# Three 192-byte gaps in SBUF ahead of stationary operands of a three-block transformer kernel

## The chip, the cores and the metric

The kernel runs on one core of one Trainium2 chip. The metric is device time in microseconds (us) from start to end of one execution; the kernel before takes 1477.13 us, the median of three runs (1477.1 to 1477.38).

## The reference, cut to what matters

The input is x, 256 tokens by 1024 channels, float32. Two layers of a first block and one second block are applied:

```
for l in 0, 1:
    x += 0.5 * rms(swiglu(rms(x), w_gu, w_down))     # 1024 -> 2*2816 -> 1024
    x += rms(hybrid_mixer(rms(x)))                   # projections, RG-LRU branch, SSD branch, gated branch, then @ w_out
    x += 0.5 * rms(swiglu(rms(x), w_gu2, w_down2))
x += (g0*y_ssm + g1*y_conv + g2*y_attn) @ w_out      # second block, "mixed" = the bracket
x += swiglu(rms(x), w_gu3, w_down3)
```

So there are five feed-forward parts, two hybrid mixers and one mixer of the second block. Every weight is read once, 480 chunks of 128 x 1024 float32.

## The kernel before, in words

Products are made in the float32r form. To keep float32 accuracy each operand is split in two, hi and lo, and a product is three matmuls: hi x hi, hi x lo, lo x hi (`product`, lines 475 to 477). SyncE brings the weight chunks in a fixed order into a ring of six slots (`raw`), ScalarE rounds each to `whi` (line 454), VectorE makes `wlo = raw - whi` (line 461), and TensorE uses them; a slot is given back by the semaphore `consumed`.

A matmul has a stationary operand, loaded into the array by a weight load (LDWEIGHTS, "PEld" in the profile), and a moving operand that streams through, up to 512 columns. The weight load of the next matmul runs beside the current matmul. In the profile's names `out<-moving,stationary` the moving operand stands first.

- Gate and up columns (`columns_of`, lines 762 and 763): the weights are stationary, the normalized input `xboth` moves. For each of 8 blocks k one matmul with 512 columns and one with 256. A hidden tile j has one gate chunk and one up chunk, so 32 matmuls; 20 tiles of each feed-forward part are made so, the first two in another form (`head`).
- Down products (`down`, `first_down`, and `held` for the last four): the hidden activations `hhi`, `hlo` are stationary (128 x 128), the weights move with 512 columns, into `acc`. 12 matmuls for a tile; 18 tiles of each part stand between gate-and-up groups, the last four make one run of 48.
- Output product of the hybrid mixer: the stationary operand is `yahi`, `yalo` for the three blocks of the recurrent branch (36 matmuls) and the two halves of `xboth` for the other five (60), `left(k, t)`; the weights move with 512 columns.
- Output product of the second block: stationary `mxhi`, `mxlo` (96 matmuls), moving weights, 512 columns.
- Token projections (`tokens`): stationary `xboth`, moving weights. Channel projections (`channels`): stationary weights, moving `xboth`, 256 columns.

The order of the work on each engine is written out by hand; the FFN tiles 6 to 17 stand in a loop of each engine, the rest is unrolled.

SBUF tensors are placed one after another in the order of their declaration. `m1` declares tensors of a scope; when a scope is closed, the next declaration starts again where that scope began. So `hhi` (first scope), `recc` (second scope) and `y5hi` (third) start at the same byte. The program's addresses in a partition, modulo 128:

```
tensor                    before   after
raw, whi, wlo, xboth         0       0
x, xn, u32                   0       0
hhi, hlo, rrow              64       0
recc, xbcc, par, xdt        64      64
yahi, yalo                  64       0
dm, yb, yc, vx               0      64
y5hi, y5lo, cvhi, cvlo      64      64
ohi, olo                    64      64
mxhi, mxlo, gsg, sgl, mt    64       0
```

Within a tensor all stationary blocks lie at multiples of 512 bytes, and a moving operand of 512 columns starts at a multiple of 1024 bytes.

Of the kernel before, what the change touches and what calls it, by code (L numbers as in the profile page):

```python
# [18 lines left out]
P = 128  # L19
# [16 lines left out]
HEADS = 6  # L36
HD = 64
VSTEPS = 49

FFN_CHUNKS = 3 * FT  # L40
MIX_CHUNKS = 30
# [164 lines left out]
def block_program(nc, stream, x_in, pf_a, pf_b, pm, pm2, out):  # L206
    ctx = ExitStack()
    with ctx:
        def sb(name, shape, dt=F32):
            return ctx.enter_context(nc.sbuf_tensor(name, shape, dt))  # L210
# [35 lines left out]
        def m1(name, shape, dt=F32):  # L246
            return scope.enter_context(nc.sbuf_tensor(name, shape, dt))

        hhi = m1("hhi", [P, HELD, S], F32R)
        hlo = m1("hlo", [P, HELD, S], F32R)  # L250
        rrow = m1("rrow", [P, S])
# [9 lines left out]
        uv = m1("uv", [P, T, 2 * CW])  # L261
        zs = m1("zs", [P, T, BW])
        xdt = m1("xdt", [P, T, BW])
        yahi, yalo = m1("yahi", [P, AB, S], F32R), m1("yalo", [P, AB, S], F32R)
        spin = m1("spin", [P, T * HEADS + AB])
        spe = m1("spe", [P, T * HEADS + AB])
# [63 lines left out]
        ohi, olo = sb("ohi", [P, 4, S], F32R), sb("olo", [P, 4, S], F32R)  # L330
        gx = sb("gx", [P, 4, S])
        gates32 += [gx[:, j, :] for j in range(3)] + [xn[:, t, 512:768] for t in range(T)] + [xn[:, 0, 768:D]]
        mxhi, mxlo = sb("mxhi", [P, KD, S], F32R), sb("mxlo", [P, KD, S], F32R)
        gsg, sgl = sb("gsg", [P, 2, 3, S]), sb("sgl", [P, 2, S])
        mt = sb("mt", [P, 3, S])
# [45 lines left out]
        def mixsig(name, per):  # L381
            mixsigs[name] = Signal(sem("m_" + name), per)
            return mixsigs[name]
# [34 lines left out]
        wst = mixsig("wst", 1)  # L418
        vstep = mixsig("vstep", VSTEPS)

# [2124 lines left out]
```

## Time and profile before

| | |
|---|---|
| median of three runs | 1477.13 us (1477.1 to 1477.38) |
| span of the profiled execution | 1475.7 us; its whole time is not listed apart, the median is 1.4 us above the span |
| PE (matmul) busy | 1459.6 us, 99%, 8583 matmuls |
| PEld (weight load) busy | 1268.2 us, 86% |
| VectorE busy | 1148.6 us, 78% |
| ScalarE busy | 766.9 us, 52% |
| granted TensorE clock | 0.995 of full speed |
| DMA | 261.75 MB, 177 GB/s |

The recorded end of a matmul is modelled and matmuls overlap in the records, so the busy time says only that TensorE never paused. What a matmul costs is read from the distance between the starts of two neighbours in the timeline.

### The profile page before, as it was taken

To read this page: it belongs to the slowest core of one execution; us is meant where nothing else is said; L and a number is where in the kernel's file an instruction comes from. 1 tells how busy PE (TensorE), PEld (TensorE's weight loads), DVE (VectorE), ACT (ScalarE), POOL (GpSimd) and SP (SyncE) were. 2 spreads that over 40 slices of the span, in tenths; PEclk is the share of its full clock that TensorE was granted. 3 is DMA by queue.
4 is the path that set the end of the run, shared out by engine and by line. 5 is a ranking of instruction groups with operands and counts; after the bars stand their busy time and mean duration, and the time that the engine had idled before them with its cause. 6 is when DMAs were issued, how large, how long until landed. Compare 5 with 4: busy or idle time off the path is not lost.

```text
span 1475.7 us, 24487 instructions
## 1 busy us (share of the span) xinstructions
PE 1459.6 (99%) x8583; PEld 1268.2 (86%) x8583; DVE 1148.6 (78%) x1831; ACT 766.9 (52%) x1252; POOL 144.1 (10%) x140
## 2 busy tenths in 40 slices
PE   8999999999999999999999999999999999999999
PEld 7888889888888888889988888889988899888887
DVE  5777777878777777777787777868999977577876
ACT  6343465663434544337655434468598665453432
POOL 0000015100000000002420000020433310000000
PEclk9999999999999999999999999999999999999999
DMA  8565545546655666655545655555522256556662
GB/s 317 195 202 190 186 168 172 161 152 194 198 183 194 213 201 201 186 188 167 159 158 182 200 197 186 198 172 182 175 72 88 87 182 187 173 164 197 195 191 80
DMA packets 71361, 261.75 MB, mean 177 GB/s; under 512 B 8048, under 2 KB 8048, under 8 KB 71024
## 3 DMA queue, kind: packets, MB, share of 16 engines
q1 hardware_dynamic: 69984, 253.79, 53.6%
q10 hardware_dynamic: 1296, 6.85, 1.3%
q8 instruction: 55, 0.90, 0.3%
q14 instruction: 26, 0.21, 0.0%
HBM read 259.56 MB, written 1.05 MB: 177 GB/s over the span
## 4 chain that ended last, share of the span: by engine, by line
PE 92%; DVE 4%; ACT 2%; issue 1%; POOL 0%; DMA 0%; ACTq 0%; DVEq 0%
PE work L762 25%; PE work L763 13%; PE acc L475 9%; PE acc L477 9%; PE acc L476 9%; PE work L475 8%; PE work L477 7%; PE work L476 7%; DVE wlo L461 2%; PE work L1494 1%; PE acc L1523 1%; ACT whi L454 1%; PE acc L1559 1%; PE work L1495 0%; PE work L1019 0%
## 5 line engine op out<-in xcount | busy, mean ns | idle before, releaser
L461 DVE TENSOR_TENSOR wlo<-raw,whi 128x1024 fp32r<-128x1024 f32 x460 | 550.8, 1224 | 179.7 <-ACT whi L454 178.6
L762 PE MATMUL work<-xboth,whi 128*128 128x512 f32 x1600 | 560.8, 394 | 0.0
L454 ACT ACTIVATE whi<-raw 128x1024 fp32r<-128x1024 f32 x480 | 475.9, 1040 | 60.9 <-PE work L477 35.9
L763 PE MATMUL work<-xboth,wlo 128*128 128x256 f32 x1600 | 444.3, 278 | 0.0
L762 PEld LDWEIGHTS work<-xboth,whi 128*128 128x128 f32 x1600 | 299.8, 187 | 69.3
L763 PEld LDWEIGHTS work<-xboth,wlo 128*128 128x128 f32 x1600 | 300.8, 188 | 4.3
L840 ACT ACTIVATE sg<-sg 128x256 f32<-128x256 f32 x100 | 41.8, 418 | 476.0 <-DVE sg L881 476.0
L477 PE MATMUL acc<-whi,hlo 128*128 128x512 f32 x440 | 173.7, 395 | 0.0
L476 PE MATMUL acc<-wlo,hhi 128*128 128x512 f32 x440 | 173.5, 394 | 0.0
L475 PE MATMUL acc<-whi,hhi 128*128 128x512 f32 x440 | 173.3, 394 | 0.0
L475 PE MATMUL work<-xboth,whi 128*128 128x256 f32 x416 | 120.1, 289 | 0.0
L476 PE MATMUL work<-xboth,whi 128*128 128x256 f32 x416 | 118.5, 285 | 0.0
L477 PE MATMUL work<-xboth,wlo 128*128 128x256 f32 x416 | 118.4, 285 | 0.0
L475 PEld LDWEIGHTS acc<-whi,hhi 128*128 128x128 f32 x440 | 82.4, 187 | 20.0
L477 PEld LDWEIGHTS acc<-whi,hlo 128*128 128x128 f32 x440 | 82.4, 187 | 19.9
L476 PEld LDWEIGHTS acc<-wlo,hhi 128*128 128x128 f32 x440 | 82.4, 187 | 15.8
L475 PEld LDWEIGHTS work<-xboth,whi 128*128 128x128 f32 x416 | 80.7, 194 | 0.5 <-issue 0.4
L476 PEld LDWEIGHTS work<-xboth,whi 128*128 128x128 f32 x416 | 80.6, 194 | 0.1
L477 PEld LDWEIGHTS work<-xboth,wlo 128*128 128x128 f32 x416 | 80.5, 194 | 0.0
L475 PE MATMUL work<-whi,xboth 128*128 128x512 f32 (+3 forms) x208 | 77.3, 371 | 2.9 <-DVE xboth L537 2.1
L543 POOL TENSOR_TENSOR prstd<-pms,small 128x1 f32<-128x1 f32 x12 | 6.6, 551 | 740.4 <-DVE pms L551 740.4
L879 DVE TENSOR_REDUCE sg<-work 128x256 f32<-128x512 f32 x100 | 68.7, 687 | 11.5 <-PE work L763 11.4
(438 smaller groups left out, 2193.5 us busy)
## 6 DMA issues: line engine op xcount, KB each, us to landing
raw<-stream SPq DMA_DIRECT2D x480, 512.0 KB, 3.7
par<-pm ACTq DMA_DIRECT2D x2, 1644.5 KB, 7.3
pfa<-pf_a ACTq DMA_DIRECT2D x3, 516.0 KB, 4.7
pfb<-pf_b ACTq DMA_DIRECT2D x2, 516.0 KB, 8.2
x<-x_in SPq DMA_DIRECT2D x2, 512.0 KB, 6.0
out<-x SPq DMA_DIRECT2D x4, 256.0 KB, 2.0
par<-pm ACTq DMA_DIRECT2D x1, 820.0 KB, 4.3
pre<-pf_a ACTq DMA_DIRECT2D x1, 4.0 KB, 4.3
```

Source lines behind the costliest of these rows:

```text
L454: nc.scalar.activation(chunk(whi, place, c)[:, cols], chunk(raw, place, c)[:, cols], ACT.Copy).then_inc(hi_ready, 1)
L461: nc.vector.tensor_tensor(chunk(wlo, place, c)[:, cols], chunk(raw, place, c)[:, cols], chunk(whi, place, c)[:, cols].bitcast(F32), ALU.su ...
L475: return [nc.tensor.matmul(o, lhi, rhi, start=start, stop=False), nc.tensor.matmul(o, lhi, rlo, start=False, stop=False), nc.tensor.matmul ...
L476: nc.tensor.matmul(o, lhi, rlo, start=False, stop=False),
L477: nc.tensor.matmul(o, llo, rhi, start=False, stop=stop)]
L762: nc.tensor.matmul(o[:, :], hi[:, k * P:(k + 1) * P], xboth[:, k, :], start=k == 0, stop=False)
L763: m = nc.tensor.matmul(o[:, 0:S], lo[:, k * P:(k + 1) * P], xhi[:, k, :], start=False, stop=k == KD - 1)
L840: nc.scalar.activation(sg[:, j % 2, :], sg[:, j % 2, :], ACT.Silu).then_inc(sg_ready, 1)
L879: nc.vector.tensor_reduce(sg[:, j % 2, :], both_halves(gate), AX.X, ALU.add).then_inc(gsum_ready, 1)
L1494: nc.tensor.matmul(bank2(f"sc{r}", slice(b * S, b * S + nkeys(t))), qT[:, h, t * P:(t + 1) * P], kT[:, 2 * b + h // 4, 0:nkeys(t)], start= ...
L1523: m = nc.tensor.matmul(acc[at:at + 32, 1, k % 2 * S:(k % 2 + 1) * S], left, rotated[:, r % 2, i // 2, i % 2, :], start=i == 0, stop=i == 3)
L1559: m = nc.tensor.matmul(acc[:, 0, at:at + HD], pT[:, r % 2, (b * 2 + k) * P:(b * 2 + k + 1) * P], xn[:, k, 768 + b * P + (h // 4) * HD:768 ...
```

## The change

Three unused tensors of 48 float32 (192 bytes in each partition) are declared, one ahead of `hhi`, one ahead of `yahi`, and one ahead of `mxhi`. No instruction is added, removed or moved; the tensors declared after a gap in the same scope (and, for the last, to the end) start 192 bytes later.

```diff
+LINE = 48
...
+        m1("hidden_line", [P, LINE])
         hhi = m1("hhi", [P, HELD, S], F32R)
         hlo = m1("hlo", [P, HELD, S], F32R)
         rrow = m1("rrow", [P, S])
...
         xdt = m1("xdt", [P, T, BW])
+        m1("lru_line", [P, LINE])
         yahi, yalo = m1("yahi", [P, AB, S], F32R), m1("yalo", [P, AB, S], F32R)
...
         gates32 += [gx[:, j, :] for j in range(3)] + [xn[:, t, 512:768] for t in range(T)] + [xn[:, 0, 768:D]]
+        sb("mixed_line", [P, LINE])
         mxhi, mxlo = sb("mxhi", [P, KD, S], F32R), sb("mxlo", [P, KD, S], F32R)
         gsg, sgl = sb("gsg", [P, 2, 3, S]), sb("sgl", [P, 2, S])
         mt = sb("mt", [P, 3, S])
```

## Rows read from the trace of the kernel before

**Rows 1.** Windows: length, then busy us (count) of each engine, clock, DMA.
```profile
core 0: us, PE busy (x) PEld busy (x) DVE busy (x) ACT busy (x) POOL busy (x), PEclk, DMA share, GB/s
22.00:195.00 173.00, 173.00 (x921) 148.40 (x921) 134.54 (x193) 73.28 (x94) 0.55 (x1) 1.00 0.61 201
```

**Rows 2.** Timeline of VectorE, one FFN tile: start us, length; idle before.
```profile
338.64 1.23 DVE L461 TENSOR_TENSOR wlo<-raw,whi 128x1024 fp32r<-128x1024 f32 x1 [1.43 <-ACT whi L454]
```

**Rows 3.** Timeline of PE: a gate-and-up group, then a down tile.
```profile
330.39 0.40 PE L762 MATMUL work<-xboth,whi 128*128 128x512 f32 x1
...
335.94 0.39 PE L475 MATMUL acc<-whi,hhi 128*128 128x512 f32 x1
336.17 0.39 PE L476 MATMUL acc<-wlo,hhi 128*128 128x512 f32 x1
...
338.74 0.40 PE L762 MATMUL work<-xboth,whi 128*128 128x512 f32 x1
```

**Rows 4.** Timeline of PE: a token projection of 48, stationary xboth; then channels.
```profile
1004.91 0.40 PE L475 MATMUL work<-whi,xboth 128*128 128x512 f32 x1
...
1006.07 0.39 PE L477 MATMUL work<-whi,xboth 128*128 128x512 f32 x1
...
1015.82 0.28 PE L475 MATMUL work<-xboth,whi 128*128 128x256 f32 x1
1015.93 0.28 PE L476 MATMUL work<-xboth,whi 128*128 128x256 f32 x1
1016.05 0.28 PE L477 MATMUL work<-xboth,wlo 128*128 128x256 f32 x1
```

**Rows 5.** Timeline of PE: last xboth matmul, then the 36 with stationary yahi, yalo.
```profile
272.97 0.39 PE L476 MATMUL work<-wlo,xboth 128*128 128x512 f32 x1
273.19 0.39 PE L477 MATMUL work<-whi,xboth 128*128 128x512 f32 x1
273.42 0.40 PE L475 MATMUL acc<-whi,yahi 128*128 128x512 f32 x1
...
281.82 1.89 PE L1056 MATMUL work<-vx,par 128*128 128x64 f32 x16
```

**Rows 6.** Timeline of PE: 39 of the matmuls with stationary mxhi, mxlo.
```profile
1263.03 0.39 PE L475 MATMUL acc<-whi,mxhi 128*128 128x512 f32 x1
...
1272.13 0.39 PE L475 MATMUL acc<-whi,mxhi 128*128 128x512 f32 x1
```

**Rows 7.** Groups of PE by form: count, busy us, mean ns of one, idle.
```profile
L475 PE MATMUL acc<-whi,hhi 128*128 128x512 f32 x440 | 173.3, 394 | 0.0
L475 PE MATMUL acc<-whi,yahi 128*128 128x512 f32 x24 | 9.5, 396 | 0.0
L475 PE MATMUL acc<-whi,mxhi 128*128 128x512 f32 x32 | 12.7, 397 | 0.0
L762 PE MATMUL work<-xboth,whi 128*128 128x512 f32 x1600 | 560.8, 394 | 0.0
```

**Rows 8.** Timeline of PE: ten matmuls of the mixer's output, from its second.
```profile
288.62 0.40 PE L476 MATMUL acc<-wlo,xboth 128*128 128x512 f32 x1
...
290.71 0.39 PE L476 MATMUL acc<-wlo,xboth 128*128 128x512 f32 x1
```

**Rows 9.** Timeline of PE: after the gated branch, a wait inside the mixer's output product.
```profile
285.14 0.47 PE L475 MATMUL acc<-whi,xboth 128*128 128x512 f32 x1 [0.76 <-DVE xboth L1326]
```

**Rows 10.** Groups by form: operands behind a gap, and two without a gap.
```profile
L1043 PE MATMUL acc<-xdt,dm 128*128 128x64 f32 x24 | 4.5, 270 | 0.0
L1065 PE MATMUL work<-ident,yb 128*128 128x128 f32 x12 | 1.6, 274 | 0.0
L1012 PE MATMUL work<-ident,xbcc 128*128 128x128 f32 x12 | 1.6, 272 | 0.0
```

**Rows 11.** Timeline of PE: up columns of the second feed-forward part, before its first down tile.
```profile
316.76 0.40 PE L762 MATMUL work<-xboth,whi 128*128 128x512 f32 x1
317.01 0.28 PE L763 MATMUL work<-xboth,wlo 128*128 128x256 f32 x1
317.13 0.40 PE L762 MATMUL work<-xboth,whi 128*128 128x512 f32 x1
317.36 0.28 PE L763 MATMUL work<-xboth,wlo 128*128 128x256 f32 x1
...
318.88 0.40 PE L762 MATMUL work<-xboth,whi 128*128 128x512 f32 x1
```

## The prediction

> **What bounds the kernel now.** I read the page's busy line first: PE is busy 99% of the span. Since the end of a matmul is modelled, this proves little alone, so I next took the windows: in 173 us of a feed-forward part PE is busy all 173.00 [rows 1], while VectorE works 134.5 us of it and ScalarE 73.3. VectorE idles 1.43 us in every tile of about 8.35 us, waiting for ScalarE's split [rows 2], so it has slack in each. So in the feed-forward parts TensorE sets the pace, and an engine that hides the effect isn't there: what a matmul gives back, the kernel gets.
>
> The third view is the timeline, read for the distance between starts. A 512-column matmul cannot start its successor earlier than its columns stream. The reader is to see three distances for the same kind of matmul (stationary 128 x 128 activations, moving weights, 512 columns, granted clock 1.00):
> - stationary `hhi`, `hlo`: a down tile starts at 335.94, its second matmul at 336.17, the next group at 338.74 [rows 3]. That is 2.80 us for 12, 0.230 for the first and 2.57 / 11 = 0.2336 for each other.
> - stationary `yahi`, `yalo`: 36 in 281.82 - 273.42 = 8.40 us, 0.2333 each [rows 5]; stationary `mxhi`, `mxlo`: 39 in 9.10 us, 0.2333 each [rows 6].
> - stationary `xboth`: the last 43 of a run of 48 take 1015.82 - 1006.07 = 9.75 us, 0.2267 each [rows 4]. Right ahead of the `yahi` matmuls, two starts lie 0.22 and 0.23 apart [rows 5].
>
> The first two groups lie 64 bytes off the weights modulo 128, `xboth` lies at 0 like them. Nothing else that I can find separates them, except that `xboth` stands at a lower address. So 6.7 ns (0.2333 - 0.2267) of each such matmul hang on the placement, and the change moves all three to 0.
>
> **The change part by part.** The gaps add no instruction, no DMA and no wait. The sum is one of matmul distances.
>
> 1. *Down tiles.* The three groups with stationary `hhi`, `hlo` have 440 each (one of them stands in [rows 7]), 1320 matmuls in all: 90 tiles of 12 and 5 runs of 48. At 0.2267 a tile takes 2.720 us instead of 2.80 (2.797 by 0.230 + 11 x 0.2333), so at most 0.077 is saved. But `xboth` doesn't start at 0.2267: the first five of the run of 48 take 1006.07 - 1004.91 = 1.16 us, 0.232 each [rows 4], a toll of 5 x 0.2320 - 5 x 0.2267 = 0.027 us. Whether a down tile, which follows gate-and-up matmuls, pays it isn't shown: bounds 0 and 0.027 per tile (0.050 for the nine at 0.232 after a pause [rows 8], see the rivals). TensorE comes from stationary weights at 0 as in the run of 48, but in another rhythm, and the first matmul already takes 0.230; I take half, 0.013. A tile saves 0.064, 90 save 5.8 us (bounds 4.5 and 6.9).
> 2. *The five runs of 48.* Each saves 47 x 0.0067 = 0.315 less 0.013, so 0.30; five save 1.5 us.
> 3. *Recurrent output.* 3 x 24 matmuls [rows 7] x 0.0067 = 0.48 us. They follow a settled `xboth` run, so no toll. But 1.9 us of gated products and the transposes come next, and then TensorE waits 0.76 us for VectorE [rows 9]. If VectorE's chain starts from TensorE's gated products, it comes earlier too; if from its own older work, the wait grows and the gain is nil. Bounds 0 and 0.48; I take 0.24.
> 4. *Mixed output.* 3 x 32 matmuls [rows 7] x 0.0067 - 0.027 = 0.6 us, with nothing waited for inside the run.
> 5. *Tensors pushed the other way.* `dm`, `yb`, `yc` and `vx` go from 0 to 64. They are stationary operands of 64 and 128 columns, where the weight load sets the distance. The nearest rows: transposes with stationary `yb` at 0 and `xbcc` at 64 take 274 and 272 ns, and the products with `dm` at 0 take 270 [rows 10]. I take 0; at 6.7 ns each, all 124 of them (72 `dm`, 32 `vx`, 20 `yb` and `yc`) would be 0.8 us either way.
> 6. `rrow`, `gsg`, `sgl`, `mt` are read by VectorE and ScalarE alone. I take nothing; both have slack, as above.
>
> Sum: 5.8 + 1.5 + 0.24 + 0.6 = 8.1 us. The profiled span is 1475.7 us and would be 1467.6; the median stands 1.4 us above the span, so the time is 1477.1 - 8.1 = 1469.0 us. Its own range: without tolls 6.9 + 1.6 + 0.5 + 0.6 = 9.6 us, 1467.5; with the whole toll everywhere and nothing for part 3, 4.5 + 1.4 + 0.6 = 6.5 us, 1470.6; with the 0.8 of part 5 either way, 1466.7 to 1471.4.
>
> **The rivals.**
>
> *Gate-and-up falls into its slower rhythm (slower).* The 512/256 pair of gate and up has two rhythms in this trace. Normally a group takes 335.94 - 330.39 = 5.55 us for 16 pairs, 0.347 a pair [rows 3]. Ahead of the first down tile of a feed-forward part, six pairs take 318.88 - 316.76 = 2.12 us, 0.353 a pair, with 0.25 in place of 0.23 at every third 512-column matmul [rows 11]. Both operands are at 0 there too, so a rhythm depends on how the group is entered, and it persists once begun. All 90 groups that follow a down tile with `hhi` at 64 show the fast one (95 of the 100 hidden tiles that the 1600 pairs [rows 7] make, since the last group of each part holds two). The change replaces exactly what comes ahead of them. If the new entry gives the slow rhythm, 0.0067 x 16 pairs = 0.107 us is lost in each of 95 tiles, 10.2 us, against 8.1 won: 1479.2 us; with the full toll on the down tiles (6.5 won) 1480.8. It decides from 76 slow tiles on. For it: of the ten 16-matmul halves made before the first down tile, five are slow. Against: channel projections that follow settled `xboth` runs come to their usual 0.12 at the second matmul [rows 4].
>
> *The tolls eat most.* If a down tile needs nine matmuls at 0.232, as the run that begins after a pause does (290.71 - 288.62 = 2.09 us for nine [rows 8]), a tile saves 2.797 - 9 x 0.232 - 3 x 0.2267 = 0.029, 90 save 2.6 us, the long runs 5 x 0.265 = 1.3, the rest 0.7: 4.6 us in all, 1472.5 us. Against: that run begins when no weight was loaded ahead, which isn't so for a down tile.
>
> *The placement isn't the cause.* Then the lower address, or the tensor's neighbourhood, makes `xboth` fast, and the distances stay: 1477.1 us. For it: `hhi`, `yahi` and `mxhi` all lie at high addresses, so phase and region aren't told apart by the rows. Against: three tensors far from each other cost the same 0.2333, and all share the phase 64.
>
> The Trainium skill speaks for this last outcome too: "TensorE: Matmul & The Clock Gate", Part 2, says that TensorE has two independent read ports of SBUF, one for the moving operand and one for the weight load, so that loading the next weights takes nothing from the running matmul. By it no placement of one against the other could matter and the time would be 1477.1 us. The trace speaks against the rule: the distance differs by which tensor is stationary while moving operand, length and clock are the same [rows 4, 5].
>
> **How the numbers follow.** The forecast of 1469.0 us (1466.7 to 1471.4) gets 0.57, the tolls (1472.5) 0.10, no effect (1477.1) 0.13, the slower rhythm 0.20. A measurement of this kernel tells about 0.2%, 3 us, from no change. Faster by more: the first two, 0.67. Slower by more is over 1480.1: the slower rhythm with tolls, half of that case, so 0.10. Within: 0.13 and the other 0.10, 0.23. The range goes from 1467.0, half a microsecond under the sum without tolls, to 1479.9, which takes in no effect and the slower rhythm's plain sum, and leaves out about 0.12.
>
> **What would show it.** In the timeline of the changed kernel the down tile should take about 2.73 us from its first matmul to the next gate matmul, with distances of 0.227 at its end; the run of 96 with `mxhi` should show 0.227 from the sixth matmul on; the mean of one recorded matmul of `acc<-whi,hhi` should fall from 394 to about 390 ns. `yahi` should change from 0.2333 to 0.2267 at once. The gate-and-up groups should keep 5.55 us: if they take 5.65, the slower rhythm is there. PE should stay at 0 idle in the feed-forward windows. I'm wrong in the cause if the distances of `hhi` stay at 0.233, wrong in the toll if a tile takes 2.77, and wrong in the cover if PE begins to wait for VectorE within a tile.

## The result

The changed kernel is slower: 1482.84 us, median of 22 runs (1477.02 to 1484.79), beside 1479.93 us (1475.77 to 1482.55) for the kernel before in 22 runs on the same chip. The ratio is 1.0019, 95% interval [1.001, 1.0027]. The first three runs of before (1477.13) lie in the lower part of that spread; all comparisons below are made with runs of before on the same chip. Two single runs far above all others, one of 2894.85 us (the kernel with only the gap ahead of `hhi`) and one of 1581.64 us (the kernel before), are left out of the ratios. The profiled execution has a span of 1479.2 us at a granted clock of 0.994 (before: 1475.7 at 0.995).

The timeline of TensorE in the changed kernel, one gate-and-up group and the down tile behind it, answers to [rows 3]:

```profile
330.13 0.39 PE L480 MATMUL acc<-wlo,hhi 128*128 128x512 f32 x1
330.36 0.39 PE L481 MATMUL acc<-whi,hlo 128*128 128x512 f32 x1
330.58 0.39 PE L766 MATMUL work<-xboth,whi 128*128 128x512 f32 x1
330.81 0.28 PE L767 MATMUL work<-xboth,wlo 128*128 128x256 f32 x1
330.92 0.40 PE L766 MATMUL work<-xboth,whi 128*128 128x512 f32 x1
331.15 0.28 PE L767 MATMUL work<-xboth,wlo 128*128 128x256 f32 x1
331.27 0.40 PE L766 MATMUL work<-xboth,whi 128*128 128x512 f32 x1
331.51 0.28 PE L767 MATMUL work<-xboth,wlo 128*128 128x256 f32 x1
331.63 0.40 PE L766 MATMUL work<-xboth,whi 128*128 128x512 f32 x1
...
336.22 0.40 PE L479 MATMUL acc<-whi,hhi 128*128 128x512 f32 x1
336.45 0.40 PE L480 MATMUL acc<-wlo,hhi 128*128 128x512 f32 x1
...
337.38 0.39 PE L481 MATMUL acc<-whi,hlo 128*128 128x512 f32 x1
...
338.74 0.39 PE L481 MATMUL acc<-whi,hlo 128*128 128x512 f32 x1
338.97 0.39 PE L766 MATMUL work<-xboth,whi 128*128 128x512 f32 x1
```

The down tile takes 338.97 - 336.22 = 2.75 us, against 2.80 before. Its first five distances are still 1.16 us in sum (336.22 to 337.38, 0.232 each), the other seven 0.227. The gate-and-up group takes 336.22 - 330.58 = 5.64 us, against 5.55. The slower rhythm is there from the start: three pairs from 330.58 take 1.05 us and each further three 1.06, 0.353 a pair, as in [rows 11]. All 90 groups that stand behind a down tile do this: the 85 single ones and the 5 double ones that end each part.

The groups by form (count, busy us, mean ns of one, idle) say the same, beside [rows 7]: `hhi` 394 to 392 ns, `yahi` 396 to 389, `mxhi` 397 to 392, and the gate-and-up matmuls 394 to 399.

```profile
L766 PE MATMUL work<-xboth,whi 128*128 128x512 f32 x1600 | 569.6, 399 | 0.0
L479 PE MATMUL acc<-whi,hhi 128*128 128x512 f32 x440 | 172.5, 392 | 0.0
L479 PE MATMUL acc<-whi,mxhi 128*128 128x512 f32 x32 | 12.6, 392 | 0.0
L479 PE MATMUL acc<-whi,yahi 128*128 128x512 f32 x24 | 9.3, 389 | 0.0
```

PE still has no idle time in the window of [rows 1]:

```profile
core 0: us, PE busy (x) PEld busy (x) DVE busy (x) ACT busy (x) POOL busy (x), PEclk, DMA share, GB/s
22.00:195.00 173.00, 173.00 (x917) 147.89 (x917) 134.34 (x192) 72.64 (x94) 0.55 (x1) 1.00 0.62 200
```

Summed over the whole trace, each matmul charged with the distance from its start to the next start:

| us | before | after | change |
|---|---|---|---|
| gate and up, 3200 matmuls | 556.40 | 564.81 | +8.41 |
| down, `hhi`, `hlo` | 307.69 | 302.45 | -5.24 |
| `mxhi`, `mxlo` | 22.74 | 22.17 | -0.57 |
| `yahi`, `yalo` | 16.80 | 16.33 | -0.47 |
| transposes of `yb`, with the wait at them | 3.18 | 3.65 | +0.47 |

That is +2.6 us, beside 2.9 us between the medians. The two profiled spans differ by 3.6 us. The rest is in the mixers (`kcT` and `qT` products +1.8, `xn` and `pT` +0.9, `y5` products -0.6), in small differences of both signs elsewhere (-0.8 in sum), and in a first matmul that starts 0.35 us earlier. The two largest of these go with the clock and not with the placement. The window of the `kcT` products, before and after:

```profile
1055.00:1067.00 12.00, 11.73 (x82) 11.23 (x82) 10.35 (x30) 4.40 (x7) 2.84 (x2) 0.86 0.29 89
1055.00:1067.00 12.00, 11.38 (x70) 10.95 (x68) 10.01 (x28) 3.72 (x7) 4.54 (x4) 0.72 0.35 108
```

The granted clock is 0.86 there before and 0.72 after: more of the window at 1.2 GHz. The `kcT` products take 3.67 us at 0.86 (before, and in the version below that reads at 0), 5.51 us at 0.72 (after) and 5.81 us at 0.57 (the version below that reads at 64). The `xn` and `pT` products take 12.12 us before and 12.99 after, where the granted clock between 1150 and 1160 us is 0.83 and not 1.00; one and the same program, that with `hlo` at 64, has 13.01 in one profile and 12.13 in another.

### The profile page after: what moved, and what is told of

It reads as the page before. It is cut to its first block, busy times and chain, and to the rows that moved or that the text cites. A ratio compares the mean times of both kernels' runs of the same rounds, so it can differ in the third digit from the quotient of the medians.

```text
span 1479.2 us, 24487 instructions
## 1 busy us (share of the span) xinstructions
PE 1462.8 (99%) x8583; PEld 1273.0 (86%) x8583; DVE 1149.4 (78%) x1831; ACT 767.3 (52%) x1252; POOL 144.1 (10%) x140
## 3 DMA queue, kind: packets, MB, share of 16 engines
q10 hardware_dynamic: 1296, 6.85, 1.3%
HBM read 259.56 MB, written 1.05 MB: 176 GB/s over the span
## 4 chain that ended last, share of the span: by engine, by line
PE 91%; DVE 5%; ACT 2%; issue 1%; POOL 0%; DMA 0%; ACTq 0%; DVEq 0%
PE work L766 25%; PE work L767 13%; PE acc L479 8%; PE acc L480 8%; PE acc L481 8%; PE work L479 8%; PE work L481 7%; PE work L480 7%; DVE wlo L465 2%; PE work L1498 1%; ACT whi L458 1%; PE acc L1527 1%; PE acc L1563 0%; PE work L1499 0%; PE work L1486 0%
## 5 line engine op out<-in xcount | busy, mean ns | idle before, releaser
L766 PE MATMUL work<-xboth,whi 128*128 128x512 f32 x1600 | 569.6, 399 | 0.0
```

What stands on the lines that cost most here:

```text
L766: nc.tensor.matmul(o[:, :], hi[:, k * P:(k + 1) * P], xboth[:, k, :], start=k == 0, stop=False)
```

## The experiments

The main reading is the same in all: the sums of distances of the gate-and-up matmuls and of those in the down products, beside the kernel before (556.40 and 307.69 us). One group of gate and up is 32 matmuls.

**Which gap does what.** First the changed kernel without the gap ahead of `hhi`, then with that gap alone.

```diff
-        m1("hidden_line", [P, LINE])
```

> The gaps ahead of yahi and mxhi stay, the one ahead of hhi is taken out. Theory (entry): the gate-and-up groups run slow because the down tile ahead of them now has its stationary operands at 0; with hhi back at 64 all 90 groups take 5.55 us again, a down tile 2.80 us, while the matmuls with yahi and mxhi keep 0.227 us: 1.0 us less than before the change (72 x 0.0067 + 96 x 0.0067 - 0.03 - what a wait eats). Rival (elsewhere): a tensor behind the other two gaps disturbs the feed-forward parts; then gate-and-up stays at 5.64 us.

Measured: 1478.91 us, ratio 0.9997 [0.9988, 1.0006]. Gate and up 556.54, down 307.82, `yahi` -0.47, `mxhi` -0.57, the wait at the `yb` transposes +0.50. The two other gaps are worth about nothing together: 1.0 us won, half of it given back at that wait.

```diff
         m1("hidden_line", [P, LINE])
-        m1("lru_line", [P, LINE])
-        sb("mixed_line", [P, LINE])
```

> Only the gap ahead of hhi. Theory (entry): gate-and-up 5.64 us a group (+0.088 in 90 groups, two tiles in five of them: +8.4 us), the 1320 down matmuls -5.2 us, so about +3.2 us against the kernel before, and yahi, mxhi back at 0.2333. Rival (elsewhere): gate-and-up 5.55 us and 5 us faster than before.

Measured: 1484.21 us, ratio 1.0023 [1.001, 1.0037]; gate and up 564.83, down 302.39, `yahi` and `mxhi` back at 16.80 and 22.74. The whole loss hangs on the place of `hhi` and `hlo`, operands that gate and up don't use.

**Which of the two operands.** The changed kernel with 64 bytes between `hhi` (0) and `hlo` (64), and the kernel before with the same 64 bytes (`hhi` 64, `hlo` 0).

```diff
         hhi = m1("hhi", [P, HELD, S], F32R)
+        m1("between_line", [P, 16])
         hlo = m1("hlo", [P, HELD, S], F32R)
```

> As after the change, with 64 more bytes between hhi and hlo: hhi at 0, hlo at 64. Two of three down matmuls have their stationary operand at 0, the last one at 64. Theory (entry, set by the last weight load): gate-and-up is entered as before the change and takes 5.55 us, the down tile lies between 2.75 and 2.80 us: 1 to 4 us faster than before. Rival (entry, set by the whole tile): mixed rhythm, gate-and-up slow at 5.64 us in all or some groups, 3 us slower or more than the kernel before.

Measured: 1476.55 us, ratio 0.9972 [0.996, 0.9983]. Gate and up keeps 5.55 us in all groups (556.14), down takes 304.91. The timeline of its down tile:

```profile
335.90 0.39 PE L480 MATMUL acc<-whi,hhi 128*128 128x512 f32 x1
...
338.67 0.39 PE L767 MATMUL work<-xboth,whi 128*128 128x512 f32 x1
```

That is 2.77 us, half of what there is to win, and the next group stays fast: this layout keeps 2.8 us of the down products' gain and pays nothing for it.

> The kernel before with 64 bytes between hhi and hlo: hhi stays at 64, hlo goes to 0. The mirror of the run with hhi at 0 and hlo at 64. Theory (the last weight loads of a down tile decide how gate-and-up is entered): the last down matmul has its stationary operand at 0 as after the change, so all 90 gate-and-up groups take 5.64 us, 8.4 us slower in sum, and the down matmuls save 1 to 3 us: 5 to 7 us slower than before. Rival (any tile with both phases in it enters well): gate-and-up 5.55 us and 1 to 3 us faster.

Measured: 1485.39 us, ratio 1.004 [1.0027, 1.0053]. The same 2.8 us are won (down 304.93), but gate and up takes 565.21, slow in all groups. So the two halves are not alike: it is `hlo` at 0 that brings the slow rhythm.

**The other operands.** `xboth` moved to 64 in the kernel before, and `wlo` moved to 64 in the version with `hlo` at 64. Each edit puts 64 bytes ahead of the tensor and 64 behind it, so all tensors declared later keep their place modulo 128 but lie 128 bytes higher.

```diff
+        sb("xboth_line", [P, 16])
         xboth = sb("xboth", [P, KD, 2 * S], F32R)
+        sb("xboth_line2", [P, 16])
```

> The kernel before with xboth alone moved to 64 (64 bytes ahead of it and 64 behind), all else at its old phase. Theory (what counts is the phase between the moving operand and the weight being loaded, 64 is worse): gate-and-up slows, by 0.0067 us for some or all of its 3200 matmuls, +5 to +21 us, and xboth as stationary operand costs 0.2333 in place of 0.2267. Rival (a moving operand at 64 against weights at 0 is better): y5hi, cvhi and ohi lie so and take 0.118 for 256 columns where xboth takes 0.120; then gate-and-up gives back 2 to 7 ns a matmul and the 1680 channel matmuls 2 ns each: 8 to 20 us faster.

Measured: 1480.56 us, ratio 1.0012 [1.0002, 1.0022]. Gate and up is slow in all groups (565.11), while the down products, whose own operands keep their phases modulo 128, go to 304.11: 0.229 us each, neither 0.227 nor 0.233. The `mxhi` products do the same, 42 distances in 9.61 us, in a run that has no operand in `xboth`:

```profile
1265.26 0.39 PE L478 MATMUL acc<-wlo,mxhi 128*128 128x512 f32 x1
...
1274.87 0.39 PE L478 MATMUL acc<-wlo,mxhi 128*128 128x512 f32 x1
```

So a matmul's pair of phases modulo 128 doesn't fix its distance. What did change for `hhi`, `yahi` and `mxhi` is the shift by 128 bytes against the weights, which stayed. The runs fit a distance that goes by the address modulo 256: `xboth` as stationary operand now lies against the weights as `hhi` did before, and its long runs settle at 0.2333, as expected. No run tests this by itself. The channel projections go from 152.87 to 149.32.

> hhi at 0, hlo at 64, and wlo moved to 64 as well (64 bytes ahead and 64 behind). Gate-and-up then loads weights at 0 and at 64 in turn. Theory (what a rhythm costs depends on the phases of all operands in the group): gate-and-up leaves 5.55 us; by the two rhythms seen with xboth at 0 it could go to 5.44 (8 cycles of 1.2 GHz less for one of two matmuls), and by the run with xboth at 64 to 5.64 or above. Rival (only activations' placement matters, since weights come in whole 4 KB slots): 5.55 us. I give no sign; 1466 to 1488 us.

Measured: 1480.09 us, ratio 0.9998 [0.9988, 1.0008]; gate and up 556.88 (5.56 us a group, so neither the 5.44 nor the 5.64 that were thought possible), down 307.23. The gain of the version with `hlo` at 64 is gone; whether by the place of `wlo` or by the shift of `hhi` and `hlo` against `whi` isn't separated.

**The order of the three matmuls.** The version with `hlo` at 64, the last matmul of each product being now `hhi` (0) with `wlo`.

```diff
+        def product_hi_last(o, lhi, llo, rhi, rlo, start, stop):
+            return [nc.tensor.matmul(o, lhi, rhi, start=start, stop=False),
+                    nc.tensor.matmul(o, llo, rhi, start=False, stop=False),
+                    nc.tensor.matmul(o, lhi, rlo, start=False, stop=stop)]
```

> hhi at 0, hlo at 64, and in the down tiles between gate-and-up groups the order of the three matmuls is hi x hi, lo x hi, hi x lo, so the stationary operands go hhi, hlo, hhi. Placement is that of the fast run, only the order differs; the last down matmul has its stationary operand at 0. Theory (the last weight loads decide): gate-and-up goes to 5.64 us in the 90 groups, about 8 us slower than the same placement in the old order. Rival (placement decides, order doesn't matter): 5.55 us stays.

Measured: 1473.59 us (4 runs), ratio 0.9954 [0.9939, 0.997]; gate and up 556.06, down 305.27. My idea that a last weight load at 0 makes the next group slow fell here: the last one is at 0 and 88 of the 90 groups are fast. The other two take 5.64 us and stand right behind the first down tile of a part; with the old order no group is slow.

> The changed kernel with its placement untouched (hhi and hlo at 0); the down products that stand between gate-and-up groups take the order hi*hi, lo*hi, hi*lo instead of hi*hi, hi*lo, lo*hi, so the last matmul has hhi and wlo. Theory (each matmul's operand pair and the rhythm that the tile settles in set the entry; with all four at 0 every matmul of the tile is alike): the tile still settles at 0.227 and gate-and-up stays at 5.64 us, 1481 to 1485 us. Rival (the order alone is what made the version with hlo at 64 fast): gate-and-up at 5.55 us, and with the down tiles' saving 1474 to 1476 us.

This is that order in the changed kernel, `hhi` and `hlo` both at 0. Measured: 1484.06 us, ratio 1.0024 [1.0014, 1.0033]; gate and up 564.81, down 302.45, both as in the changed kernel to the hundredth. With both operands at 0 the order does nothing.

**A phase between.** The gap of the changed kernel cut to 96 bytes, so that `hhi` and `hlo` lie at 32.

```diff
-        m1("hidden_line", [P, LINE])
+        m1("hidden_line", [P, 24])
```

> As after the change, with a gap of 96 in place of 192 bytes ahead of hhi: hhi and hlo at 32. Theory (lines of 64 bytes count: 32 behaves as 0): down matmuls settle at 0.2267 us and gate-and-up is slow, 5.64 us. Rival (any phase but 0 behaves as 64): 0.2333 us and 5.55 us, as before the change. A third outcome, a distance between the two, would say that the phase counts in finer steps.

Measured: 1484.49 us, ratio 1.0033 [1.002, 1.0046]; down 307.73, gate and up 560.81. The timeline (first matmul of each group and tile) shows why the second number lies halfway:

```profile
322.59 0.40 PE L766 MATMUL work<-xboth,whi 128*128 128x512 f32 x1
...
328.15 0.39 PE L479 MATMUL acc<-whi,hhi 128*128 128x512 f32 x1
...
330.94 0.40 PE L766 MATMUL work<-xboth,whi 128*128 128x512 f32 x1
...
336.58 0.40 PE L479 MATMUL acc<-whi,hhi 128*128 128x512 f32 x1
...
339.38 0.40 PE L766 MATMUL work<-xboth,whi 128*128 128x512 f32 x1
...
344.93 0.39 PE L479 MATMUL acc<-whi,hhi 128*128 128x512 f32 x1
```

5.56, then 5.64, then 5.55 us: fast and slow groups take turns through every part, with all operands in the same phases. The alternation isn't tied to the tile's number, and so not to its PSUM banks: three parts begin with a fast group and end with a slow double one, two begin slow and end fast, tile for tile with the same banks. The two that begin slow are those whose half group ahead of the first down tile took 2.86 us, in the other three it took 2.90 or 2.91. So with `hlo` at 32 what a group does goes with the group ahead, across the down tile. Neither expectation is met: the distances are those of 64, the groups those of neither.

**Another entry.** In the changed kernel, once the first gate matmul of a group and once the last matmul of a down tile is issued as two of 256 columns.

```diff
+                    if split and k == 0:
+                        for s in (slice(0, S), slice(S, 2 * S)):
+                            nc.tensor.matmul(o[:, s], hi[:, 0:P], xboth[:, 0, s], start=s.start == 0, stop=False)
```

> The changed kernel with its placement untouched; only the first gate matmul of each group (block k = 0, 512 columns) is issued as two of 256 columns with the same stationary operand, so that the group is entered in another state. Theory (the slow gate-and-up rhythm is handed over by the state in which the group is entered, and persists): the groups leave 5.640 us for about 5.56 to 5.59 (5.55 and up to 0.03 for the extra matmul); gate-and-up loses most of its +8.4 us, the time is 1476 to 1479 us. Rival (the placement of hhi and hlo as such, or what lies beside them, makes gate-and-up slow): they stay at 5.64 or go to 5.67, and the time is 1482 to 1486 us. The down tiles keep 0.227 at their end by both.

> The changed kernel with its placement untouched; only the last matmul of each down tile (llo * rhi, 512 columns) is issued as two of 256 columns. The tile ends in another state, and gate-and-up itself is not edited. Theory (entry state): the groups leave 5.640 us, all or part of them, for 5.55; down tiles take 2.75 to 2.78 us; 1476 to 1480 us. Rival (placement as such): 5.64 in all groups, 1482 to 1486 us. If the extra matmul hands over the same state, 5.64 stays too, and only the version with the split gate matmul decides.

Measured: 1483.39 us, ratio 1.0023 [1.0007, 1.0038], and 1487.88 us, ratio 1.0052 [1.0037, 1.0067]. The groups take 5.65 us in both, in the first with the extra matmul in the group, in the second with it in the tile ahead: slow in both. My theory said that either would free them. It missed twice. By then a second rule fitted all kernels but the alternating one and the two groups above: gate and up is slow where `hlo` has the phase of `xboth` modulo 128, which could be an effect of how VectorE writes `hlo`.

**Reading or writing.** The down tiles read their stationary operands from another tensor than the one that VectorE writes: in the kernel before from `xboth` (read at 0, `hhi` and `hlo` written at 64), in the changed kernel from a fixed tensor (read at 64, written at 0). The down result is another one.

```diff
-                        m = product(acc[:, t, cols], hhi[:, j % 4, t * P:(t + 1) * P], hlo[:, j % 4, t * P:(t + 1) * P],
+                        m = product(acc[:, t, cols], xboth[:, j % 4, t * P:(t + 1) * P], xboth[:, j % 4, S + t * P:S + (t + 1) * P],
```

> The kernel before (hhi, hlo written at 64 as always), but the down tiles between gate-and-up groups read their stationary operands from xboth (at 0) in place of hhi, hlo; so the down result is another one, number and kinds of matmuls are the same. Theory A (the phase at which TensorE reads the stationary operand of the down tile sets the rhythm handed over): down tiles at 0.227, gate-and-up slow, 5.64 us a group in all 90; 1478 to 1485 us. Theory B (the phase at which hhi and hlo are written, against that of xboth): gate-and-up keeps 5.55 us, and down tiles at 0.227 give 1471 to 1475 us.

Measured: 1481.8 us, ratio 1.0022 [1.0007, 1.0037]; all 90 groups slow (564.78 in sum). The timeline:

```profile
331.06 0.39 PE L762 MATMUL work<-xboth,whi 128*128 128x512 f32 x1
...
336.70 0.40 PE L475 MATMUL acc<-whi,xboth 128*128 128x512 f32 x1
...
339.45 0.39 PE L762 MATMUL work<-xboth,whi 128*128 128x512 f32 x1
```

> The counterpart: the changed kernel (hhi, hlo written at 0), but the down tiles read their stationary operands from a tensor at 64 that is written once at the start and not changed; the down result is another one, number and kinds of matmuls are the same. Theory A: down tiles at 0.233, gate-and-up fast, 5.55 us in all groups; about 1477 to 1480 us. Theory B: gate-and-up slow, 5.64 us, with down tiles at 0.233; 1484 to 1489 us.

Measured: 1479.3 us, ratio 0.9999 [0.9983, 1.0014]; all 90 groups fast (556.52):

```profile
330.46 0.39 PE L769 MATMUL work<-xboth,whi 128*128 128x512 f32 x1
...
336.02 0.39 PE L482 MATMUL acc<-whi,still 128*128 128x512 f32 x1
```

Same phase of writing, other phase of reading, and the rhythm follows the reading. The rule about the writes falls, and the same rule about the reads stands. From where TensorE loads the stationary operand of the down tile decides how fast the matmuls behind that tile run, for 5.6 us after its last use. (The tensors that are read hold other values too; the changed kernel, with the same values, says that these aren't what counts.)

**Without a tile that settles.** Each later down tile cut to one matmul, 11 of 12 are left out, with `hlo` at 0 and at 64.

```diff
-                for t in range(T):
-                    for h in range(2):
...
+                m = nc.tensor.matmul(acc[:, 0, cols], hlo[:, j % 4, 0:P], hi[:, cols], start=False, stop=False)
```

> The changed kernel with each later down tile cut to its one matmul hlo * whi of 512 columns (11 of 12 are left out). Theory A (the tile's settled 0.227 rhythm is what slows the next group): without such a run the groups are handed over from gate-and-up to gate-and-up, so one rhythm stays through a whole feed-forward part, slow or fast as its first groups (entered behind transposes) are, not the same in all parts: 5.55 in some parts, 5.64 in others. Theory B (the phases of hlo and xboth as such): 5.64 in all groups.

> The same cut in the kernel before (hlo at 64). Theory A: as with hlo at 0, one rhythm through each part, not the same in all. Theory B: 5.55 in all groups, 0.1 us a group less than with hlo at 0.

Measured: 1472.25 and 1467.1 us, one run each. By the distances of its last pairs, 68 of 100 runs of gate and up end in the slow rhythm with `hlo` at 0, and 61 of 100 with `hlo` at 64, so neither expectation is met: not all alike, and not one rhythm through a part, since TensorE now pauses for VectorE's split before most groups (80 waits, 108 us in sum, with `hlo` at 64). With `hlo` at 64:

```profile
33.54 0.39 PE L762 MATMUL work<-xboth,whi 128*128 128x512 f32 x1
...
39.09 0.40 PE L778 MATMUL acc<-whi,hlo 128*128 128x512 f32 x1
39.32 0.39 PE L762 MATMUL work<-xboth,whi 128*128 128x512 f32 x1
...
44.97 0.39 PE L778 MATMUL acc<-whi,hlo 128*128 128x512 f32 x1
46.66 0.47 PE L762 MATMUL work<-xboth,whi 128*128 128x512 f32 x1 [1.31 <-DVE wlo L461]
...
511.04 0.40 PE L762 MATMUL work<-xboth,whi 128*128 128x512 f32 x1
...
516.60 0.40 PE L778 MATMUL acc<-whi,hlo 128*128 128x512 f32 x1
```

The group from 33.54 takes 5.55 us, the one from 39.32 takes 5.65, with one matmul and no pause between them. So `hlo` at 64 alone doesn't guard the fast rhythm. This place comes once in each of the five parts: in three the group turns slow as here, in two it stays fast (5.56 us from 511.04). That in the full kernel the whole tile in the 0.233 rhythm guards it is my reading and isn't shown. The windows row shows the next bound:

```profile
22.00:195.00 173.00, 146.28 (x741) 121.74 (x741) 135.68 (x195) 74.56 (x99) 0.55 (x1) 0.94 0.62 202
```

PE falls from 173.0 to 146.3 us of work in the window while VectorE's work stays (135.7), and the kernel gains only 12 us (1478.9, the median of 14 runs of before, to 1467.1): behind TensorE the chain from ScalarE's split to VectorE's split is close. Part of this is TensorE's own: with its pauses the granted clock is 0.94 in the window and 0.958 over the run, where the kernel before has 1.00 and 0.995.

**The best version.** The `hlo` at 64 layout with the other order in the runs of 48 and the output products too, then both versions again on one chip.

> The version with 64 bytes between hhi and hlo (hhi 0, hlo 64) and the order hi*hi, lo*hi, hi*lo in the down tiles, with that order now in the run of 48 of each feed-forward part and in the three output products too. Theory: gate-and-up stays at 5.55 us in all groups; where all stationary operands are at 0 (xboth, yahi, mxhi) the order changes nothing, in the five runs of 48 with hhi, hlo at most 0.3 us in sum: 1472 to 1475 us, below the kernel before (about 1479.9) by 0.3 to 0.5%. Rival (the state at the end of a long run reaches into what follows): the channel and token projections or the transposes behind the runs change by over 1 us.

Measured: 1476.1 us, ratio 0.998 [0.9968, 0.9992], just above what was expected; gate and up 556.18 (87 of 90 groups fast), down 305.19. The order in the long runs changes nothing.

> The version with hhi at 0, hlo at 64 and the order hi*hi, lo*hi, hi*lo in the down tiles, a second time. If its first result held (ratio 0.9954 to the kernel before), 0.994 to 0.997. If the order adds nothing to the layout, as the sums of matmul distances say (gate-and-up 5.547 in place of 5.550 us, 0.3 us in all; down tiles within 0.4 us), 0.9965 to 0.998 and within 1 us of the layout alone.

> The layout alone (hhi at 0, hlo at 64, the order of the kernel before), on the same chip: 0.9965 to 0.998; gate-and-up 5.550 us in all groups.

Measured: 1476.75 us, ratio 0.9977 [0.9968, 0.9986], with the order, and 1477.43 us, 0.9978 [0.9968, 0.9988], with the layout alone; gate and up 556.18 and 556.21, down 305.26 and 304.95. The order adds nothing that shows; its first result, four runs on another chip with nearly the same sums (556.06 and 305.27), is best read as a low draw. The layout alone is worth 0.22%, some 3.3 us, over the kernel before, where the whole change loses 0.19%. The sum of distances gave 3.5: 2.7 down, 1.0 output products, 0.2 gate and up, less 0.5 at the `yb` wait.

## Why the prediction was wrong

The time came out at 1482.8 (1479.9 before on that chip) where 1469.0 was forecast from 1477.1: +0.2% for -0.55%. Point by point:

1. *Placement sets the distance.* Right in direction: `hhi`, `yahi` and `mxhi` go to 0.227, a kernel without their gap takes each back to 0.233, and "the placement isn't the cause" is refuted. The Trainium skill's sentence on two independent read ports ("TensorE: Matmul & The Clock Gate", Part 2) would have left all distances alone; the trace disagrees by 6.7 ns on each 512-column matmul. But "64 or 0 modulo 128" is too simple: with `xboth` at 64, and `hhi` thereby 128 bytes higher, the `hhi`, `whi` pair takes 0.229.
2. *Down tiles, -5.8 us, and the runs of 48, -1.5.* Mis-sized: -5.2 together against 7.3. I took half the toll; it is paid in full in each tile (five at 0.232), so a tile saves 0.049 and not 0.064, 4.4 us for 90. The runs of 48 pay it over about ten matmuls (2.33 us for the first ten, 0.063 more than at 0.2267), which leaves 0.25 each, 1.2 in all. Charged with the next start it is 0.17 each, since in three of them what follows now starts 0.11 us later; the `rdiag` transposes there give the same 0.36 us back (7.22 to 6.85).
3. *Recurrent output, -0.24.* The bound of nil was the right one: 0.47 won in the matmuls, 0.47 more at the `yb` transposes, without a toll, as foreseen.
4. *Mixed output, -0.6.* -0.57.
5. *Tensors pushed the other way, 0.* The sums of the `dm` and `vx` products and of the `yc` transposes don't move by 0.01 us. (`vx` is the moving operand there, `work<-vx,par`, and not the stationary one, as the prediction had it.)
6. *Gate and up keep 5.55 us.* This is the step that failed, worth +8.4 us against the 5.8 that all other terms together brought. The rival "gate-and-up falls into its slower rhythm", with a chance of 0.20, is what happened: its price was 0.107 a tile in 95 tiles, 10.2 us; measured were 5.640 - 5.552 = 0.088 for each of the 85 single groups and 11.290 - 11.099 = 0.19 for each of the five double ones, 8.4 in all; the ten halves ahead of the first down tiles take 28.96 us in sum in both kernels. The rival priced every pair at 0.353 against 0.347, but the first pairs of a slow group still cost less. The 6.5 us won with the full toll was 6.3, so the rival's 3.7 us of loss was 2.1, and with the `yb` wait 2.6.

What misled me stands in the argument against that rival: channel projections that follow a settled `xboth` run come to 0.12 at once [rows 4]. That shows that the toll is absent, not which of two rhythms follows, since in 0.12 a difference of 3 ns can't be read. The better evidence was in [rows 11]: the same matmuls, the same operands, two rhythms, and the fast one seen in 90 groups that all stand behind the same kind of tile. With half of the other entries slow and the one kind of entry about to be replaced in all 90 places, one half was the honest chance and not one fifth.

What is shown: the place from which TensorE reads the stationary operands of the down tile sets the rhythm of the following group (the change itself, and the pair that separates reading from writing). Both rhythms exist at one placement (`hlo` at 32, and the tile cut to one matmul), and in every kernel with whole tiles a rhythm, once begun behind a down tile, lasts through its group. Behind a tile that settled at 0.227 gate and up was slow in every kernel; behind one at 0.233 it was fast in three (the kernel before, the one without the gap ahead of `hhi`, the one that reads at 64) and alternating in the fourth (`hlo` at 32). What stays open is what is handed over, and why `hhi` 0, `hlo` 64 is fast and the reverse slow: the phase of the last weight load (the other order), the last distance (0.233 ahead of groups of 5.55 us in the kernel before and of groups of 5.64 us with `hhi` 64, `hlo` 0) and a shift by one matmul are each excluded as the sole cause. That addresses count modulo 256 in the distances is likely and untested.

## What to carry to other kernels

A gain read from the distance between matmuls holds for the run in which it was measured; before it is multiplied by a count, ask whether the next run of matmuls has more than one rhythm in the trace, and take the change as able to switch it in every repetition at once. Where an address changes, time each neighbour's group, not only the one that uses the address. And try single operands: half of the change (`hhi` at 0, `hlo` at 64) won what the whole lost.

## What the runs showed of the hardware that was not expected

- Gate and up, 512 then 256 columns, has two steady rhythms: 0.3467 us a pair (5.55 us for a group) and 0.3533 (5.64). The choice is made at the entry and lasts, in one case 64 matmuls (11.10 or 11.29 us).
- The choice depends on the byte address of stationary operands of the matmuls ahead, in a run that is over: read at 64 modulo 128, 90 of 90 groups at 5.55 us, read at 0, 90 of 90 at 5.64. At 32 it goes with the group ahead, across 2.8 us of other matmuls.
- 512-column matmuls settle at 0.2267, 0.229 or 0.2333 us, at a granted clock of 1.00, and two placements that are equal modulo 128 and 128 bytes apart differ (0.2333 and 0.229 for `mxhi`); the 0.2267 rhythm needs five to ten matmuls at about 0.232 to settle, unless it is taken over from a run that has it.
- Moving `xboth` by 64 bytes made the channel projections (256 columns, `xboth` moving) faster, 152.87 to 149.32 us for 1248 matmuls, in the kernel that lost 8.7 us in gate and up.
- Of two profiles of nearly the same program the mixers can differ by 2 us through the granted clock alone: `kcT` products 3.67 us in a window at 0.86, 5.51 at 0.72, 5.81 at 0.57.
